# Pre-norm factors moved from the weights to the transposed inputs in a two-layer hybrid decoder kernel, and the high/low weight split made two tiles at a time

## The chip, the core and the metric

The kernel runs on one core of a Trainium2 chip, as one launch. The time is device microseconds (us) of that launch, and the median of several runs is compared. Five engines work beside each other and meet at semaphores: TensorE (PE, matmuls; PEld are its weight loads), VectorE (DVE), ScalarE (ACT), GpSimd (POOL) and SyncE (SP, which here issues the DMAs).

## What is computed

Two layers run one after the other over 256 tokens of 1024 features, all in fp32. A layer has four sub-layers: a SwiGLU FFN, a token mixer (retention heads and gated-linear-attention heads side by side), cross-attention into 256 memory tokens, and a second SwiGLU FFN. Each one is wrapped in two RMSNorms:

```
def rmsnorm(x, g):
    y = x * rsqrt(mean(x * x, axis=-1) + EPS)
    return y * g                          # g: one factor per feature

for l in range(2):
    x = x + 0.5 * rmsnorm(swiglu(rmsnorm(x, ffn1_pre_g[l]), ...), ffn1_post_g[l])
    x = x + rmsnorm(hybrid_mixer(rmsnorm(x, mix_pre_g[l]), ...), mix_post_g[l])
    x = x + rmsnorm(memory_cross_attn(rmsnorm(x, xa_pre_g[l]), rmsnorm(mem, xa_mem_g[l]), ...), xa_post_g[l])
    x = x + 0.5 * rmsnorm(swiglu(rmsnorm(x, ffn2_pre_g[l]), ...), ffn2_post_g[l])
```

The change is about the factors `g` of the norms that stand ahead of a projection: `ffn1_pre_g`, `mix_pre_g`, `xa_pre_g`, `xa_mem_g`, `ffn2_pre_g`, and the per-head norm factors that stand ahead of the mixer's output projection (`G_HEAD`). Since rmsnorm(x, g) @ W is r * (x @ (g * W)) and also r * ((x * g) @ W), with r one number per token, a factor can be multiplied into the rows of W or into the columns of x.

## The kernel before

**Numbers in two parts.** fp32 operands are written as a high part (rounded to the format fp32r) and a low part (the rest), and every product is three matmuls: high x low, low x high and high x high (`three`, L463 to L467). So every weight that streams in is split by two instructions: ACT writes `w_hi` (`split_hi`, L833) and DVE writes `w_lo` = weight minus `w_hi` (`split_lo`, L1153). The same is done to every transposed input: PE transposes 128x128 blocks of x into a PSUM bank `tb` (`transposes`, L516), ACT copies the bank into `xT_hi` (`t_hi`, L864), DVE subtracts and writes `xT_lo` (`t_lo`, L1174).

**Weights.** They come in chunks of 512 output columns by up to 8 blocks of 128 rows, in two halves (h = 0, 1) of 4 blocks (k = 0..3). Four half-sized slots (`raw`, `w_hi`, `w_lo`) are used in turn; SP loads a slot as soon as its split is done. For a chunk behind a norm the factors are in the split: ACT copies each block with a per-partition scale (L858) and DVE multiplies and subtracts in one instruction (L1170), one block of 128x512 at a time, since the factor differs from block to block. For a chunk with no norm ahead of it (FFN down, the attention's output) the split is two blocks at a time, 128x1024 (`pieces`, L852 and L1164). PE waits on `s_lo` for each block, or each pair of blocks.

**Order.** Each engine has one queue written out by hand. PE runs passes: one pass is one chunk by one tile of 128 tokens (t = 0, 1), 24 matmuls of 512 columns. At the seams between sub-layers two chunks are run as a `pair` (L546): first both with t = 0, then both with t = 1, so that tile 0 can start while tile 1 still is being normed. `boundary` (L888 on ACT, L1209 on DVE) is the order there: the square sum of the output (`y_square`), the residual update of tile 0 (`x_update`, L1206), the split of the next chunk's first half, then the copies of the transposed tile 0 (`x_hi`, `x_lo`), then on ACT the square of x (`x_square`, `junk_x` L878) and the second half, then the same for tile 1. POOL does the small per-token arithmetic of the norms in order: `pre` (five to seven operations on 128x1, L1600 to L1607) for the next norm of tile 0, and behind it `post` (L1590 to L1593) for the residual update of tile 1.

**Mixer.** The levels of the gated attention are a chain: POOL forms exponents and decayed keys (L1644, L1645, L1657, L1658), ACT takes the exponential, PE multiplies (`level`, L593), DVE takes the result out (`level_out`). Weight splits stand between them in DVE's queue. For the low-rank gate `w_ga` the factor is multiplied in by an instruction of its own (`w_ga_s`, L1338) ahead of its split.

**Memory.** Behind the mixer's output chunk are the square sum of the memory tokens (L1060), their norm (POOL L1679 and L1680, DVE L1420), and their transposes and copies (`mem_hi`, `mem_lo`).

Of the kernel before, what the change touches and what calls it, by code (L numbers as in the profile page):

```python
# [33 lines left out]
ds = bass.ds  # L34
# [25 lines left out]
def ffn_chunks(f):  # L60
    gain = (G_FFN1, G_FFN2)[f]
    up = [(f"gu{f}", j, 0, 4, gain) for j in range(FU)]
    return up + [(f"down{f}", n, k, nk, None) for n, k, nk in DOWN]
# [4 lines left out]
CHUNKS += [("in", c, 0, 4, G_MIX) for c in range(6)]  # L68
C_OUT = len(CHUNKS)
CHUNKS += [("out", c, 0, 4, G_HEAD) for c in range(2)]  # L70
C_K = len(CHUNKS)
CHUNKS += [("kv", c, 0, 4, G_MEM) for c in range(2)]
C_Q = len(CHUNKS)
CHUNKS += [("q", c, 0, 4, G_XA) for c in range(2)]
C_V = len(CHUNKS)
CHUNKS += [("kv", 2 + c, 0, 4, G_MEM) for c in range(2)]
C_O = len(CHUNKS)
CHUNKS += [("o", c, 0, 4, None) for c in range(2)]
# [44 lines left out]
N_TS = len(SPLIT_USES)  # L123

# [8 lines left out]
def program(nc, a, out):  # L133

    ctx = ExitStack()
    with ctx:
# [29 lines left out]
        w_ga_s = sb("w_ga_s", [P, KD, RANK])  # L166
# [102 lines left out]
        s_tev = sem("transposed_evacuated")  # L269
        s_m = [sem(f"mixer_bank_done{i}") for i in range(2)]  # L270
# [12 lines left out]
        s_gas = sem("w_ga_scaled")  # L283
# [48 lines left out]

        def m_no(l, use):
            return l * N_M + M_USES.index(use) + 1
# [32 lines left out]
        def other(l):  # L367

            return l * -1 + 1

        def weight_src(ci, h, l, j=None):
# [4 lines left out]
            name, col, k0, nk, _ = CHUNKS[ci]  # L376
# [78 lines left out]
        def _(pe):  # L455
# [4 lines left out]
            def wait_split(use, l):  # L460
                pe.wait_ge(s_tev, t_no(l, use) + 1)
# [7 lines left out]
            def token_pass(l, ci, q, t, src_hi, src_lo, k_src=0, first=True, last=True, x_ci=0, x_q=0,  # L469
# [3 lines left out]
                nk, gained = CHUNKS[ci % N_CH][3], CHUNKS[ci % N_CH][4] is not None  # L473
# [3 lines left out]
                for h in range(2):  # L477
# [21 lines left out]
            def column_pass(l, ci, q, t, src_hi, src_lo):  # L499

                wait_acc(l, q, t)
                for mt in range(2):
                    c = (2 * t + mt) * P
                    for h in range(2):
                        slot = (2 * ci + h) % 4
                        for k in range(4):
                            if t == 0 and mt == 0:
                                pe.wait_ge(s_lo, 4 * half_no(l, ci, h) + k + 1)
# [323 lines left out]
        def _(act):  # L832
            def split_hi(l, ci, h, i=None):  # L833

                lay = l
                if ci >= N_CH:
                    lay = other(l)
                _, _, _, nk, gain = CHUNKS[ci % N_CH]
# [25 lines left out]
            def t_hi(l, use, dst, cols=COL, extra=0):  # L864
                act.wait_ge(s_t, t_no(l, use) + 1 + extra)
                act.activation(dst, tb[t_bank(use)][:, 0:cols], ACT.Copy).then_inc(s_thi, 1)

            def x_hi(l, phase, t):
                for g in range(2):
                    t_hi(l, ("x", phase, t, g), xT_hi[:, 4 * g:4 * g + 4, t * P:(t + 1) * P])  # L870
# [102 lines left out]
            def mixer(l):  # L973
# [18 lines left out]
                act.wait_ge(s_gas, l + 1)  # L992
                act.activation(w_ga_hi[:, :, :], w_ga_s[:, :, :], ACT.Copy).then_inc(s_gah, 1)
# [44 lines left out]
                def mix_hi(t):  # L1038
                    for g in range(2):
                        t_hi(l, ("mix", t, g), xT_hi[:, 4 * g:4 * g + 4, t * P:(t + 1) * P])  # L1040
# [7 lines left out]
            def mem_hi(l, t):  # L1048
                for g in range(2):
                    t_hi(l, ("mem", t, g), mT_hi[:, 4 * g:4 * g + 4, t * P:(t + 1) * P])  # L1050
# [84 lines left out]
            for h in range(2):  # L1135
                act.wait_ge(s_raw[h], 16)
                for k in range(4):
                    g = G_FFN1 * KD + 4 * h + k
                    act.activation(w_hi[:, h, k, :], raw[:, h, k, :], ACT.Copy,
                                   scale=gains[:, g:g + 1]).then_inc(s_hi, 1)  # L1140
# [11 lines left out]
        def _(dve):  # L1152
            def split_lo(l, ci, h, i=None):  # L1153

                lay = l
                if ci >= N_CH:
                    lay = other(l)
                _, _, _, nk, gain = CHUNKS[ci % N_CH]
                slot = (2 * ci + h) % 4
                before = 4 * half_no(l, ci, h) + (0 if i is None else i * 16)  # L1160
                if gain is None:
                    for a, b in pieces(nk):
                        dve.wait_ge(s_hi, before + a + 2)
                        dve.tensor_tensor(w_lo[:, slot, a:b, :], raw[:, slot, a:b, :],  # L1164
                                          w_hi[:, slot, a:b, :].bitcast(F32), ALU.subtract).then_inc(s_lo, 2)
                    return
# [639 lines left out]
```

## Time and profile before

| | us |
|---|---|
| three runs | 1245.61, 1245.77, 1248.5 |
| median | 1245.77 |
| the profiled execution: span from the first to the last instruction | 1248.1 |
| its own time (the span and what lies around it) | of the runs only 1248.5 is longer than this span |
| PE busy | 1221.2 (98%) |
| DVE busy | 803.7 (64%) |
| ACT busy | 670.3 (54%) |
| POOL busy | 156.0 (12%) |
| granted TensorE clock, mean | 0.990 |
| chain that ended last | PE 89%, DVE 4%, issue 2%, POOL 2%, ACT 1% |

A matmul's record overlaps the next one's, so "busy" for PE says that its queue had work and not how fast it went; that is read from the distance of the starts. An engine that isn't PE matters only where PE waits for it. The granted clock is at its upper level (1.0, 2.4 GHz) or its lower one (0.50, 1.2 GHz).

### The profile page before, as it was taken

The numbers are of one execution on the slowest core, as the hardware profiler recorded it, in microseconds if no ns is written. First come the engines' busy times: TensorE is split into PE (matmuls) and PEld (weight loads), VectorE is DVE, ScalarE is ACT, GpSimd is POOL, SyncE is SP. The second block draws the span as 40 slices with busy tenths as digits, with TensorE's granted clock in tenths as the row PEclk, the third lists the DMA queues.
The fourth block names the chain that finished last, engine by engine and source line by source line (L and its number), as shares of the span: only waits on it lengthen the run. The fifth ranks groups of instructions, "written<-read, shape, count | busy, mean of one in ns | idle before, by whom it ended". The sixth has DMA issues, their size and how long they took to land.

```text
span 1248.1 us, 19438 instructions
## 1 busy us (share of the span) xinstructions
PE 1221.2 (98%) x6120; PEld 1022.5 (82%) x6120; DVE 803.7 (64%) x1214; ACT 670.3 (54%) x1117; POOL 156.0 (12%) x282
## 2 busy tenths in 40 slices
PE   7999999999999999999999999999999999999997
PEld 5888888787898888888888888877879988888886
DVE  6767546766756576665476665467667556767655
ACT  6555436644655465553465554456457446555444
POOL 1000003642210010000010000037322001000001
PEclk9999999999999999999999999999899999999999
DMA  8556564333553355565465565463345544555563
GB/s 332 202 174 213 193 210 155 135 111 129 184 201 127 123 192 193 177 211 189 157 204 188 182 210 189 157 211 110 102 169 165 167 159 135 203 174 196 181 213 129
DMA packets 32916, 220.06 MB, mean 176 GB/s; under 512 B 4272, under 2 KB 4528, under 8 KB 8768
## 3 DMA queue, kind: packets, MB, share of 16 engines
q1 hardware_dynamic: 32544, 218.98, 51.2%
q8 instruction: 46, 0.75, 0.2%
q14 instruction: 38, 0.31, 0.1%
q10 hardware_dynamic: 288, 0.02, 0.0%
HBM read 217.93 MB, written 1.05 MB: 175 GB/s over the span
## 4 chain that ended last, share of the span: by engine, by line
PE 89%; DVE 4%; issue 2%; POOL 2%; ACT 1%; DMA 0%; DVEq 0%; ACTq 0%; POOLq 0%
PE acc L465 27%; PE acc L467 27%; PE acc L466 26%; PE tb L524 3%; DVE w_lo L1170 2%; PE mb L610 2%; PE acc L762 1%; PE mb L746 1%; PE mb L699 1%; ACT w_hi L858 1%; DVE xT_lo L1176 0%; POOL r_head L1667 0%; DMA inv_f<-in_inv_freq 0%; DVE pg L1304 0%; DVE w_lo L1164 0%
## 5 line engine op out<-in xcount | busy, mean ns | idle before, releaser
L1170 DVE SCALAR_TENSOR_TENSOR w_lo<-raw,gains,w_hi 128x512 fp32r<-128x512 f32 x580 | 418.1, 782 | 47.2 <-ACT w_hi L858 46.1
L465 PE MATMUL acc<-w_hi,xT_hi 128*128 128x512 f32 x1024 | 411.5, 402 | 7.9 <-DVE xT_lo L1176 3.5
L467 PE MATMUL acc<-w_hi,xT_lo 128*128 128x512 f32 x1024 | 402.4, 393 | 0.0
L466 PE MATMUL acc<-w_lo,xT_hi 128*128 128x512 f32 x1024 | 401.6, 392 | 0.0
L858 ACT ACTIVATE w_hi<-raw,gains 128x512 fp32r<-128x512 f32 x580 | 370.0, 714 | 40.7 <-PE acc L467 40.4
L465 PEld LDWEIGHTS acc<-w_hi,xT_hi 128*128 128x128 f32 x1024 | 194.4, 190 | 51.4 <-DVE xT_lo L1176 5.7
L467 PEld LDWEIGHTS acc<-w_hi,xT_lo 128*128 128x128 f32 x1024 | 193.9, 189 | 42.2
L466 PEld LDWEIGHTS acc<-w_lo,xT_hi 128*128 128x128 f32 x1024 | 194.5, 190 | 38.0
L1164 DVE TENSOR_TENSOR w_lo<-raw,w_hi 128x1024 fp32r<-128x1024 f32 x112 | 123.5, 1145 | 72.6 <-ACT w_hi L852 71.9
L923 ACT ACTIVATE th<-acc,r_half 128x256 f32<-128x256 f32 x88 | 41.9, 476 | 197.1 <-PE acc L467 195.3
L852 ACT ACTIVATE w_hi<-raw 128x1024 fp32r<-128x1024 f32 x112 | 105.4, 991 | 77.2 <-PE acc L467 77.2
L465 PE MATMUL acc<-w_hi,hT_hi 128*128 128x512 f32 x352 | 139.3, 396 | 0.0
L467 PE MATMUL acc<-w_hi,hT_lo 128*128 128x512 f32 x352 | 137.9, 392 | 0.0
L466 PE MATMUL acc<-w_lo,hT_hi 128*128 128x512 f32 x352 | 136.8, 389 | 0.0
L1241 DVE SCALAR_TENSOR_TENSOR gt<-th,acc 128x256 f32<-128x256 f32 x88 | 37.0, 421 | 138.8 <-ACT th L923 138.5
L1590 POOL TENSOR_TENSOR v_post<-yss 128x1 f32<-128x1 f32 x16 | 3.1, 194 | 825.5 <-ACT junk_y L885 825.3
L467 PEld LDWEIGHTS acc<-w_hi,hT_lo 128*128 128x128 f32 x352 | 66.1, 188 | 15.4
L466 PEld LDWEIGHTS acc<-w_lo,hT_hi 128*128 128x128 f32 x352 | 66.1, 188 | 14.3
L465 PEld LDWEIGHTS acc<-w_hi,hT_hi 128*128 128x128 f32 x352 | 66.2, 188 | 13.1
L1196 DVE TENSOR_TENSOR yg<-acc,post_gain 128x512 f32<-128x512 f32 x32 | 21.7, 688 | 46.8 <-ACT junk_y L885 46.8
L885 ACT ACTIVATE junk_y<-acc 128x512 bf16<-128x512 f32 x32 | 19.0, 593 | 53.7 <-PE acc L467 53.4
L1244 DVE SCALAR_TENSOR_TENSOR h_tok<-gt,c_half,acc 128x256 f32<-128x256 f32 x88 | 42.3, 481 | 3.1
(175 smaller groups left out, 1264.3 us busy)
## 6 DMA issues: line engine op xcount, KB each, us to landing
raw<-in_gu SPq DMA_DIRECT2D x92, 1024.0 KB, 5.1
raw<-in_down SPq DMA_DIRECT2D x32, 1024.0 KB, 5.0
raw<-in_in SPq DMA_DIRECT2D x24, 1024.0 KB, 5.1
raw<-in_kv SPq DMA_DIRECT2D x16, 1024.0 KB, 5.1
raw<-in_down SPq DMA_DIRECT2D x16, 768.0 KB, 4.2
raw<-in_out SPq DMA_DIRECT2D x8, 1024.0 KB, 5.2
raw<-in_q SPq DMA_DIRECT2D x8, 1024.0 KB, 5.1
raw<-in_o SPq DMA_DIRECT2D x8, 1024.0 KB, 5.1
```

The lines of the kernel that those rows point to most:

```text
L465: pe.matmul(o, st_hi, mv_hi, start=first, stop=False)
L466: pe.matmul(o, st_hi, mv_lo, start=False, stop=False)
L467: return pe.matmul(o, st_lo, mv_hi, start=False, stop=last)
L524: mm = pe.transpose(tb[t_bank(use)][0:rows, lo:lo + w], src, ident[:, :])
L610: mm = pe.matmul(mb[e][:, c:c + 64], tile, later, start=True, stop=True)
L852: act.activation(w_hi[:, slot, a:b, :], raw[:, slot, a:b, :], ACT.Copy).then_inc(s_hi, 2)
L858: act.activation(w_hi[:, slot, k, :], raw[:, slot, k, :], ACT.Copy, scale=gains[:, ds(g, 1)]).then_inc(s_hi, 1)
L923: act.activation(th[:, t, :], acc[(q0 + j) % 2][t][:, 0:256], ACT.Tanh, scale=r_half[:, t:t + 1]).then_inc(s_tanh, 1)
L1164: dve.tensor_tensor(w_lo[:, slot, a:b, :], raw[:, slot, a:b, :], w_hi[:, slot, a:b, :].bitcast(F32), ALU.subtract).then_inc(s_lo, 2)
L1170: dve.scalar_tensor_tensor(w_lo[:, slot, k, :], raw[:, slot, k, :], gains[:, ds(g, 1)], w_hi[:, slot, k, :].bitcast(F32), ALU.mult, ALU.su ...
L1241: dve.scalar_tensor_tensor(gt[:, t, :], th[:, t, :], 1.0, b[:, 0:256], ALU.add, ALU.mult).then_inc(s_gated, 1)
L1244: dve.scalar_tensor_tensor(h_tok[:, j % 2, t, :], gt[:, t, :], c_half[:, t:t + 1], b[:, 256:512], ALU.mult, ALU.mult).then_inc(s_accf[bank ...
```

## The change

The factors leave the weights. A transposed input now goes through three instructions where there were two: DVE multiplies the PSUM bank by the factors into a part of the buffer `yg` (`gained`), ACT copies that into the high part (`gained_hi`), DVE subtracts (`gained_lo`). DVE does both banks of a tile first and both subtractions after (`gained_pair`). ACT's copy waits for DVE's multiplication and not for PE any more. All weight splits are now without factors and two blocks at a time. PE waits for inputs on a new semaphore (`s_split`), and for the weights in pairs of blocks. `w_ga_s` is gone. The second layer's factors of the first FFN are chosen by `x_gain`.

```diff
@@ tensor @@
-                pe.wait_ge(s_tev, t_no(l, use) + 1)
+                if use in GAIN_USES or use[:3] == ("x", 0, 0):
+                    pe.wait_ge(s_split, tg_no(l, use) + 1)
+                else:
+                    pe.wait_ge(s_tev, t_no(l, use) + 1)
...
-                        if t == 0 and (gained or k in (0, 2)):
-
-                            step = k + 1 if gained else k + 2
-                            pe.wait_ge(s_lo, 4 * half_no(l, ci, h) + 4 * x_ci + step)
+                        if t == 0 and k in (0, 2):
+
+                            pe.wait_ge(s_lo, 4 * half_no(l, ci, h) + 4 * x_ci + k + 2)
@@ scalar @@
-                if gain is None:
-                    for a, b in pieces(nk):
-                        act.activation(w_hi[:, slot, a:b, :], raw[:, slot, a:b, :], ACT.Copy).then_inc(s_hi, 2)
-                    return
-
-                act.nop(nofuse=True)
-                for k in range(nk):
-                    g = lay * (N_GAINS * KD) + gain * KD + h * nk + k
-                    act.activation(w_hi[:, slot, k, :], raw[:, slot, k, :], ACT.Copy,
-                                   scale=gains[:, ds(g, 1)]).then_inc(s_hi, 1)
+                for a, b in pieces(nk):
+                    act.activation(w_hi[:, slot, a:b, :], raw[:, slot, a:b, :], ACT.Copy).then_inc(s_hi, 2)
...
+            def gained_hi(l, use, dst):
+
+                act.wait_ge(s_tev, t_no(l, use) + 1)
+                act.activation(dst, xg(use), ACT.Copy).then_inc(s_thi, 1)
@@ vector @@
-                for k in range(nk):
-                    dve.wait_ge(s_hi, before + k + 1)
-                    g = lay * (N_GAINS * KD) + gain * KD + h * nk + k
-                    dve.scalar_tensor_tensor(w_lo[:, slot, k, :], raw[:, slot, k, :], gains[:, ds(g, 1)],
-                                             w_hi[:, slot, k, :].bitcast(F32), ALU.mult,
-                                             ALU.subtract).then_inc(s_lo, 1)
+                for a, b in pieces(nk):
...
+            def gained(l, use, kind):
...
+                dve.wait_ge(s_t, t_no(l, use) + 1)
+                dve.tensor_tensor(xg(use), tb[t_bank(use)][:, :].rearrange("p (k n) -> p k n", k=4),
+                                  gains[:, col].unsqueeze(2).to_broadcast([P, 4, P]), ALU.mult).then_inc(s_tev, 1)
+
+            def gained_lo(l, use, dst, hi):
+
+                dve.wait_ge(s_thi, ts_no(l, use) + 1)
+                dve.tensor_tensor(dst, xg(use), hi.bitcast(F32), ALU.subtract).then_inc(s_split, 1)
+
+            def gained_pair(l, uses, kind, dst, hi, t):
+                for use in uses:
+                    gained(l, use, kind)
+                for use in uses:
+                    g = use[-1]
+                    s = (slice(None), slice(4 * g, 4 * g + 4), slice(t * P, (t + 1) * P))
+                    gained_lo(l, use, dst[s], hi[s])
...
             def x_lo(l, phase, t):
-                for g in range(2):
-                    s = (slice(None), slice(4 * g, 4 * g + 4), slice(t * P, (t + 1) * P))
-                    t_lo(l, ("x", phase, t, g), xT_lo[s], xT_hi[s])
+                gained_pair(l, [("x", phase, t, g) for g in range(2)], x_gain(l, phase), xT_lo, xT_hi, t)
...
-                g_mix = gains[:, ds(l * (N_GAINS * KD) + G_MIX * KD, KD)].unsqueeze(2).to_broadcast([P, KD, RANK])
-                dve.tensor_tensor(w_ga_s[:, :, :], w_ga[:, ds(l, 1), :, :].rearrange("p o k n -> p (o k) n"), g_mix,
-                                  ALU.mult).then_inc(s_gas, 1)
...
             def mix_out(l):
...
                 mem_lo(l, 1)
+
+                dve.wait_ge(s_split, tg_no(l, ("mem", 1, 1)) + 1)
                 y_gain(l, 1, Q_OUT, 0, 1)
```

At the seam from the first FFN to the mixer, ACT's queue before has this behind the first half of the next chunk (`tb` is the PSUM bank, `junk_x` the square of x that POOL's `pre` waits for):

```order
L866 ACTIVATE xT_hi<-tb 128x4x128 [waits transposed]
...
L878 ACTIVATE junk_x,xss<-x 128x1024 [waits x_squared,x_ready]
L849 REGISTER_ALU [waits raw_loaded3]
L858 ISA [waits pass_done]
L858 ACTIVATE w_hi<-raw,gains 128x512
...
L885 ACTIVATE junk_y,yss<-acc 128x512 [waits y_squared,pass_done]
```

and after the change:

```order
L876 ACTIVATE xT_hi<-yg 128x4x128 [waits transposed_evacuated]
...
L888 ACTIVATE junk_x,xss<-x 128x1024 [waits x_squared,x_ready]
L862 REGISTER_ALU [waits raw_loaded3]
L864 ACTIVATE w_hi<-raw 128x1024 [waits pass_done]
L864 ACTIVATE w_hi<-raw 128x1024
L867 REGISTER_ALU
L895 ACTIVATE junk_y,yss<-acc 128x512 [waits y_squared,pass_done]
```

The copy of the transposed tile (left out: the second one of the same form) keeps its place and now waits for DVE's `transposed_evacuated`; the square of x stays behind it. DVE's queue at the same seam before, from the copies of tile 0 to the residual update of tile 1:

```order
L1176 TENSOR_TENSOR xT_lo<-tb,xT_hi 128x4x128 [waits transposed_hi_copied]
...
L1170 ISA [waits w_hi_ready]
L1170 SCALAR_TENSOR_TENSOR w_lo<-raw,gains,w_hi 128x512
...
L1196 TENSOR_TENSOR yg<-acc,post_gain 128x512 [waits y_squared]
L1201 REGISTER_ALU
L1206 SCALAR_TENSOR_TENSOR x<-yg,r_post,x 128x512 [waits acc_free1,r_post_ready]
```

and after the change:

```order
L1182 TENSOR_TENSOR yg<-tb,gains 128x512
...
L1188 TENSOR_TENSOR xT_lo<-yg,xT_hi 128x4x128 [waits transposed_hi_copied]
...
L1168 TENSOR_TENSOR w_lo<-raw,w_hi 128x1024 [waits w_hi_ready]
...
L1213 TENSOR_TENSOR yg<-acc,post_gain 128x512 [waits y_squared]
...
L1223 SCALAR_TENSOR_TENSOR x<-yg,r_post,x 128x512 [waits acc_free1,r_post_ready]
```

Two instructions (one for each bank) now stand ahead of the two subtractions, and four weight instructions became two. Between the mixer and its output projection DVE's queue after the change reads as follows; before, the `yg<-tb,gains` rows weren't there and each `w_lo` row stood for half as many blocks:

```order
L1352 TENSOR_TENSOR o_sb<-o_sb,gate 128x512 [waits heads_normed,acc_free1]
...
L1168 TENSOR_TENSOR w_lo<-raw,w_hi 128x1024 [waits w_hi_ready]
...
L1182 TENSOR_TENSOR yg<-tb,gains 128x512 [waits transposed]
...
L1188 TENSOR_TENSOR xT_lo<-yg,xT_hi 128x4x128 [waits transposed_hi_copied]
...
L1430 TENSOR_SCALAR mem_t<-mem_t,r_mem 128x1024 [waits r_mem_ready]
```

## Rows read from the trace of the kernel before

**Rows 1.** The page's first part: busy time, share of the span and instructions.
```profile
PE 1221.2 (98%) x6120; PEld 1022.5 (82%) x6120; DVE 803.7 (64%) x1214; ACT 670.3 (54%) x1117; POOL 156.0 (12%) x282
```

**Rows 2.** PE's waits: waited for; us in total, times, longest (one of eight).
```profile
PE acc L465 <- DVE xT_lo L1176: 3.5, 2, 1.8
```

**Rows 3.** Timeline, FFN up: start, us, engine line op out<-in, count.
```profile
60.24 0.39 PE L467 MATMUL acc<-w_hi,xT_lo 128*128 128x512 f32 x1
60.47 0.39 PE L465 MATMUL acc<-w_hi,xT_hi 128*128 128x512 f32 x1
```

**Rows 4.** Timeline, split without factors, 128x1024, on DVE and on ACT.
```profile
128.44 2.36 DVE L1164 TENSOR_TENSOR w_lo<-raw,w_hi 128x1024 fp32r<-128x1024 f32 x2
...
127.28 2.00 ACT L852 ACTIVATE w_hi<-raw 128x1024 fp32r<-128x1024 f32 x2
```

**Rows 5.** Timeline, the start; in brackets the idle time and its releaser.
```profile
8.48 1.29 DVE L1176 TENSOR_TENSOR xT_lo<-tb,xT_hi 128x512 fp32r<-128x512 f32 x2
...
10.48 0.79 PE L465 MATMUL acc<-w_hi,xT_hi 128*128 128x512 f32 x1 [3.48 <-DVE w_lo L1551]
```

**Rows 6.** Timeline, seam from the first FFN to the mixer.
```profile
196.38 1.06 ACT L878 ACTIVATE junk_x<-x 128x1024 bf16<-128x1024 f32 x1
...
198.28 2.74 DVE L1170 SCALAR_TENSOR_TENSOR w_lo<-raw,gains,w_hi 128x512 fp32r<-128x512 f32 x4 [0.96 <-ACT w_hi L858]
...
199.15 0.60 POOL L1604 TENSOR_SCALAR r<-r_pre 128x1 f32<-128x1 f32 x1
...
202.79 1.41 DVE L1206 SCALAR_TENSOR_TENSOR x<-yg,r_post,x 128x512 f32<-128x512 f32 x2 [1.17 <-POOL r_post L1593]
204.12 2.73 DVE L1170 SCALAR_TENSOR_TENSOR w_lo<-raw,gains,w_hi 128x512 fp32r<-128x512 f32 x4
...
205.22 0.39 PE L465 MATMUL acc<-w_hi,xT_hi 128*128 128x512 f32 x1
```

**Rows 7.** Timeline, inside the mixer.
```profile
235.18 8.80 DVE L1170 SCALAR_TENSOR_TENSOR w_lo<-raw,gains,w_hi 128x512 fp32r<-128x512 f32 x8
...
239.15 0.72 PE L602 MATMUL mb<-gqk 64*128 64x128 f32 x8 [0.22 <-POOL gqk L1658]
...
244.46 1.57 PE L610 MATMUL mb<-gqk 64*128 64x64 f32 x16 [1.62 <-DVE pgx L1293]
```

**Rows 8.** Timeline, from the mixer to the output projection and the memory tokens.
```profile
302.63 2.72 DVE L1170 SCALAR_TENSOR_TENSOR w_lo<-raw,gains,w_hi 128x512 fp32r<-128x512 f32 x4
...
306.01 0.50 PE L465 MATMUL acc<-w_hi,xT_hi 128*128 128x512 f32 x1 [1.77 <-DVE xT_lo L1176]
...
310.48 2.56 ACT L858 ACTIVATE w_hi<-raw,gains 128x512 fp32r<-128x512 f32 x4
...
315.98 1.09 PE L524 MATMUL tb<-ident,mem_t 128*128 128x128 f32 x8 [0.61 <-DVE mem_t L1420]
```

**Rows 9.** Timeline: attention to second FFN, then from layer 0 to layer 1.
```profile
442.86 3.40 DVE L1170 SCALAR_TENSOR_TENSOR w_lo<-raw,gains,w_hi 128x512 fp32r<-128x512 f32 x5
...
444.80 0.39 PE L465 MATMUL acc<-w_hi,xT_hi 128*128 128x512 f32 x1
...
630.65 2.73 DVE L1170 SCALAR_TENSOR_TENSOR w_lo<-raw,gains,w_hi 128x512 fp32r<-128x512 f32 x4
...
632.03 0.39 PE L465 MATMUL acc<-w_hi,xT_hi 128*128 128x512 f32 x1
...
634.53 2.74 DVE L1170 SCALAR_TENSOR_TENSOR w_lo<-raw,gains,w_hi 128x512 fp32r<-128x512 f32 x4 [1.15 <-ACT w_hi L858]
```

**Rows 10.** Timeline of DVE at the end of the program.
```profile
1243.57 1.42 DVE L1206 SCALAR_TENSOR_TENSOR x<-yg,r_post,x 128x512 f32<-128x512 f32 x2 [0.88 <-POOL r_post L1593]
```

**Rows 11.** Stretches: PE, PEld, DVE, ACT, POOL busy (instructions), granted clock, DMA share, GB/s.
```profile
243.10:246.50 3.40, 2.04 (x21) 2.00 (x22) 2.33 (x5) 1.42 (x3) 3.25 (x5) 1.00 0.60 186
246.50:249.90 3.40, 3.40 (x13) 2.81 (x11) 3.24 (x5) 2.76 (x5) 3.32 (x5) 0.50 0.50 212
304.60:308.00 3.40, 1.99 (x9) 1.64 (x10) 3.37 (x7) 3.29 (x6) 0.00 (x0) 1.00 1.03 429
```

More of the change, by code:

```diff
@@ L60, in ffn_chunks @@
 def ffn_chunks(f):
-    gain = (G_FFN1, G_FFN2)[f]
-    up = [(f"gu{f}", j, 0, 4, gain) for j in range(FU)]
-    return up + [(f"down{f}", n, k, nk, None) for n, k, nk in DOWN]
+    up = [(f"gu{f}", j, 0, 4) for j in range(FU)]
+    return up + [(f"down{f}", n, k, nk) for n, k, nk in DOWN]
 CHUNKS = ffn_chunks(0)
 C_IN = len(CHUNKS)
-CHUNKS += [("in", c, 0, 4, G_MIX) for c in range(6)]
+CHUNKS += [("in", c, 0, 4) for c in range(6)]
 C_OUT = len(CHUNKS)
-CHUNKS += [("out", c, 0, 4, G_HEAD) for c in range(2)]
+CHUNKS += [("out", c, 0, 4) for c in range(2)]
 C_K = len(CHUNKS)
-CHUNKS += [("kv", c, 0, 4, G_MEM) for c in range(2)]
+CHUNKS += [("kv", c, 0, 4) for c in range(2)]
 C_Q = len(CHUNKS)
-CHUNKS += [("q", c, 0, 4, G_XA) for c in range(2)]
+CHUNKS += [("q", c, 0, 4) for c in range(2)]
 C_V = len(CHUNKS)
-CHUNKS += [("kv", 2 + c, 0, 4, G_MEM) for c in range(2)]
+CHUNKS += [("kv", 2 + c, 0, 4) for c in range(2)]
 C_O = len(CHUNKS)
-CHUNKS += [("o", c, 0, 4, None) for c in range(2)]
+CHUNKS += [("o", c, 0, 4) for c in range(2)]
 C_FFN2 = len(CHUNKS)
@@ L123 @@
 N_TS = len(SPLIT_USES)
+GAIN_USES = [u for u in SPLIT_USES if u[0] != "h"]
+N_TG = len(GAIN_USES)
 LEVELS = [128, 64, 32, 16, 8, 4, 2, 1]
@@ L282, in program @@
         s_rope_t = sem("rope_table_ready")
-        s_gas = sem("w_ga_scaled")
         s_gah = sem("w_ga_hi_ready")
@@ L329, in ts_no, with x_gain, xg, tg_no @@
             return l * N_TS + SPLIT_USES.index(use) + 2
+        def x_gain(l, phase):
+            return (l, (G_FFN1, G_MIX, G_XA, G_FFN2)[phase]) if phase < 4 else (other(l), G_FFN1)
+        def xg(use):
+            t = 1 if use[0] == "mem" else use[-2]
+            return yg[:, t, use[-1] * COL:(use[-1] + 1) * COL].rearrange("p (k n) -> p k n", k=4)
+        def tg_no(l, use):
+            if use[0] == "x" and use[1:3] == (0, 0):
+                return l * N_TG + use[3]
+            return l * N_TG + GAIN_USES.index(use) + 2
         def m_no(l, use):
@@ L833, in split_hi @@
             def split_hi(l, ci, h, i=None):
[L835 to L838, printed above, removed]
+                nk = CHUNKS[ci % N_CH][3]
                 slot = (2 * ci + h) % 4
@@ L991, in split_after @@
                         split_hi(l, ci + 2, 0)
-                act.wait_ge(s_gas, l + 1)
-                act.activation(w_ga_hi[:, :, :], w_ga_s[:, :, :], ACT.Copy).then_inc(s_gah, 1)
+                act.activation(w_ga_hi[:, :, :], w_ga[:, ds(l, 1), :, :].rearrange("p o k n -> p (o k) n"),
+                               ACT.Copy).then_inc(s_gah, 1)
                 split_hi(l, C_IN + 1, 1)
@@ L1136, in _ @@
                 act.wait_ge(s_raw[h], 16)
[L1137 to L1140, printed above, removed]
+                for k0, k1 in pieces(4):
+                    act.activation(w_hi[:, h, k0:k1, :], raw[:, h, k0:k1, :], ACT.Copy).then_inc(s_hi, 2)
             x_square(0, 0, 0)
@@ L1153, in split_lo @@
             def split_lo(l, ci, h, i=None):
[L1155 to L1158, printed above, removed]
+                nk = CHUNKS[ci % N_CH][3]
                 slot = (2 * ci + h) % 4
                 before = 4 * half_no(l, ci, h) + (0 if i is None else i * 16)
[L1161 to L1166, printed above, removed]
-                for k in range(nk):
-                    dve.wait_ge(s_hi, before + k + 1)
-                    g = lay * (N_GAINS * KD) + gain * KD + h * nk + k
-                    dve.scalar_tensor_tensor(w_lo[:, slot, k, :], raw[:, slot, k, :], gains[:, ds(g, 1)],
-                                             w_hi[:, slot, k, :].bitcast(F32), ALU.mult,
-                                             ALU.subtract).then_inc(s_lo, 1)
+                for a, b in pieces(nk):
+                    dve.wait_ge(s_hi, before + a + 2)
+                    dve.tensor_tensor(w_lo[:, slot, a:b, :], raw[:, slot, a:b, :],
+                                      w_hi[:, slot, a:b, :].bitcast(F32), ALU.subtract).then_inc(s_lo, 2)
             def t_lo(l, use, dst, hi, extra_t=0, extra_s=0):
@@ L1412, in mem_lo @@
             def mem_lo(l, t):
-                for g in range(2):
-                    s = (slice(None), slice(4 * g, 4 * g + 4), slice(t * P, (t + 1) * P))
-                    t_lo(l, ("mem", t, g), mT_lo[s], mT_hi[s])
+                gained_pair(l, [("mem", t, g) for g in range(2)], (l, G_MEM), mT_lo, mT_hi, t)
             def mix_out(l):
@@ L1546, in _ @@
             x_lo(0, 0, 0)
-            for h in range(2):
-                for k in range(4):
-                    dve.wait_ge(s_hi, 4 * h + k + 1)
-                    g = G_FFN1 * KD + 4 * h + k
-                    dve.scalar_tensor_tensor(w_lo[:, h, k, :], raw[:, h, k, :], gains[:, g:g + 1],
-                                             w_hi[:, h, k, :].bitcast(F32), ALU.mult, ALU.subtract).then_inc(s_lo, 1)
+            split_lo(0, 0, 0)
+            split_lo(0, 0, 1)
             split_lo(0, 1, 0)
```

31 lines of the change are left out of this document (16 added, 15 removed).

## The prediction

> **What bounds the kernel now.** Read the page's first part first: PE is busy for 98% of the span, DVE for 64%, ACT for 54% [rows 1]. Then see whether PE really runs: in an FFN's up stage its matmuls start 0.23 us apart [rows 3], and that distance holds through all FFN passes; no wait of PE falls in them. So the weight splits there, most of DVE's and ACT's work, lie beside PE and are worth nothing. What is left is PE's idle time, 27 us of 1248, and it has places: the start, where 3.48 us end with the first split [rows 5], the inside of the mixer [rows 7], and the way from the mixer to the memory tokens [rows 8]; PE's list of waits says the same, with 1.8 us twice for a transposed tile [rows 2]. The third thing to read is how near the other seams are to a wait. At the seam from the first FFN to the mixer the first block of the pass that starts at 205.22 is split by about 204.9 [rows 6]: 0.35 us of cover. At the layer's end it is 631.4 against 632.03, and ahead of the second FFN 443.6 against 444.80 [rows 9].
>
> **The change, part by part.** The steady state first. Four blocks of a half chunk take DVE 2.73 us now [rows 6] and 2.36 in two pieces [rows 4]; ACT 2.56 [rows 8] and 2.00 [rows 4]. Over the 588 factored blocks that is about 54 us of DVE and 80 us of ACT less, all under PE's passes: 0 us. What remains is the added step of each transposed tile, and the first piece, which is ready 1.22 us after its start instead of 0.75 (a two-piece row's 2.36 less a pitch of 1.14). The added multiplication is priced by the subtraction it resembles, two in 1.29 us [rows 5], 0.64 each.
>
> What a tile's path does now: ACT and DVE overlap on two banks. After: both multiplications on DVE, then ACT's copies, then both subtractions. More important, ACT's copies now stand behind whatever DVE has queued, and everything behind them on ACT waits too. For each place I lay the queues out again with these durations.
>
> *Start.* DVE is free at 8.4. Two multiplications end at 9.7, ACT's second copy (0.6) at 10.4, ACT's first weight piece (1.05) at 11.3, DVE's first piece 1.22 later at 12.6. PE begins at 12.7 instead of 10.48 [rows 5]: **+2.2**. Nothing behind it catches up, since PE is the bound.
>
> *Seam to the mixer, once a layer.* Tile 0 itself is early enough. But ACT's square of x, at 196.38 [rows 6], can start only behind the copies: DVE ends the first half's split at 196.0, multiplies until 197.3, ACT copies until 197.8, so +1.4. POOL's chain for the next norm hangs on that square, and POOL's chain for the residual update of tile 1 stands behind it. While DVE splits, POOL's operations on 128x1 take 0.60 each [rows 6] where undisturbed ones take 0.19; with two pieces of 1.14 fewer of them are caught, but each for longer, and the last runs later: another +0.3. So the update moves from 202.79 to about 204.5, the split behind it from 204.12 to 205.83, and its first piece is ready at 207.05 where PE wants it at 205.22: 1.83 of wait. Tile 1's copies, for which PE now loses 0.3 at 212, then come in time, since the next half chunk is split earlier (ACT no longer waits for `w_ga_s`). Net 1.55, twice: **+3.1**.
>
> *Mixer.* Eight factored blocks take DVE 8.80 us there, 1.1 each instead of 0.68, because POOL works on its exponents at the same time [rows 7]. The Trainium skill, page "SBUF — State Buffer", section "SBUF: two separate sides", says that VectorE with two SBUF inputs and GpSimd take a shared port pair in turn, each for a whole instruction. The trace agrees as far as the 1.1 goes. If instead both were merely slowed in proportion, the shorter splits would release the later PE wait some 0.8 us sooner, and the whole sum would be 1.6 lower.
>
> By taking turns, counted in the mixer's queues: POOL's first decayed keys come 0.6 later (PE waits for them at 239.15), the splits end 0.9 sooner, and PE's wait at 244.46 then ends on POOL at about 244.3. Net -0.15, twice: **-0.3**.
>
> *Mixer to memory tokens, once a layer.* DVE splits from 302.63. In two pieces that ends at 304.9; multiplications until 306.2; ACT's first copy in between until 306.25; the subtraction until 307.0. PE starts at 307.05 instead of 306.01 [rows 8]: +1.04. Then gate, product, split and tile 1: DVE's multiplications end at 312.5, ACT's copies at 313.1, so ACT's next split starts there and not at 310.48, and is 0.56 shorter. The memory's square sum, norm and transposes follow it: PE transposes at 318.05 instead of 315.98. Together +2.05 a layer, twice: **+4.1**. Behind it the queues run 1 us late, but the column passes cover that.
>
> *Attention to the second FFN.* The square of x is 1.3 later, but POOL was free for 0.3 of it: the update is 1.0 later, the first piece ready at 445.1 against 444.80: +0.35, twice: **+0.7** (bounds 0 and 0.9).
>
> *Layer 0 to layer 1, once.* As in the seam to the mixer: first piece at 630.65 + 1.7 + 1.22 = 633.6 against 632.03 [rows 9]: 1.6. The next split waits 1.15 us in the loop's return, now at 634.53 and then at 636.2, which moves as the branch does; it covers itself but for 0.2. Tile 1's multiplications come behind it, and its last subtraction ends 1.0 after PE wants it (0.16 now). **+2.7**.
>
> *End.* The last residual update is at 1243.57 [rows 10], behind the same ACT and POOL chain: **+1.75**. The output's DMA and the last splits follow.
>
> Sum: 2.2 + 3.1 - 0.3 + 4.1 + 0.7 + 2.7 + 1.75 = 14.25 us.
>
> **The clock.** In the stretch from 243.1 to 246.5 PE is busy for 2.04 us of 3.40, mostly with 64-column matmuls, and in the next one the granted clock is 0.50: 13 matmuls in 3.4 us. In 304.6 to 308.0 it is busy for 1.99 us and the clock stays at 1.0 [rows 11]. Such half-speed stretches (1.2 GHz) stand at the same three places of both layers and cost about 1.5 us each. The change lengthens the idle at 304 to 307 from 1.8 to 2.8 us, makes new waits of 1.6 to 1.9, and delays the first matmuls at the start, where PE also runs at half clock until 14.4. Bounds for the net: three fewer (-4.5) and five more (+7.5). I take one more, +1.5, since PE's idle grows and nowhere shrinks by much, and rows 11 show that 1.4 us of idle alone was not enough. The sum becomes 15.75.
>
> The page "TensorE: Matmul & The Clock Gate" of the Trainium skill, section "Part 1: The HAM clock gate", says the activity monitor runs free of the program's start. By that rule the same idle time costs in one run and not in another. No row here shows it, and one trace cannot.
>
> The sum stands against the profiled execution (span 1248.1, near the run of 1248.5). The median of the runs is 2.3 below that span; the added waits don't depend on which of them is meant, so I add them to the median: 1245.8 + 15.75 = 1261.5, said as **1262**.
>
> **The rivals.**
> - *The clock follows every longer wait.* Five more half-speed stretches instead of one: 14.25 + 7.5, 1267.5. For it: the idle of 2.8 us at 304, and four new waits of 1.6 and more. Against it: at 304 to 307 PE is caught up later by the memory's wait anyway. Chance 0.15.
> - *Only the two multiplications count.* If POOL and ACT do not carry the delay on to tile 1, each of eight seams and ends costs the 1.3 us added on DVE less the 0.4 to 0.5 saved in the split: about 7, so 1253. For it: cover of 0.35 to 1.2 at three of four kinds of seam. Against it: the order above puts the square of x behind the copies. Chance 0.13.
> - *Nothing moves.* Each added step lies in slack I did not see: within 3.7 us of 1245.8. It is also where a change that moved no wait would land. Against it: the start alone costs 2.2, with nothing ahead of PE. Chance 0.06.
> - *Faster: the mixer decides.* There a wait of 1.62 us, 0.22 ahead of it, and a half-speed stretch of 1.5 hang on DVE's and POOL's turns. If shorter splits freed both, 3.3 us a layer come back, 6.6 in all: 1239 if the seams cost nothing. It decides only when the seams cost under 6.6 together, against the 14.5 above. Chance 0.04.
> - The forecast, 1257 to 1266: 0.62.
>
> **The range.** 1252 to 1270 takes in the rival of the multiplications, the bounds of the small terms, and most of the clock's. What a measurement of this kernel can tell from no change is about 0.3%, 3.7 us. Faster than that 0.04, within it 0.07, slower 0.89.
>
> **What would show it.** Right: PE's first matmul of the first pass near 12.7; a PE wait of 1.8 for `w_lo` in the second pass behind each first FFN; the wait for the transposed tile at the output projection grown from 1.77 to 2.8 and the one for `mem_t` from 0.6 to near 1.9; FFN passes still at 0.23 us a matmul; the last residual update 1.7 later behind PE's last matmul. Wrong: if the seam's wait is absent, POOL's chain did not carry the delay; if the excess is in stretches with a granted clock of 0.50, the clock is the cause and not the queues; if the FFN passes are slower than 0.23, the longer instructions take something from PE that no row shows.

## The result

The changed kernel takes 1261.38 us (median of 4 runs, 1259.46 to 1261.93), the kernel before 1247.13 beside it (1245.61 to 1251.11): ratio 1.0102, interval 1.0074 to 1.0129. It is slower by 14.25 us. The forecast was 1262, range 1252 to 1270.

The page of the changed kernel gives, as [rows 1] for before:

```profile
PE 1219.0 (97%) x6120; PEld 1018.7 (81%) x6120; DVE 776.8 (62%) x968; ACT 592.1 (47%) x823; POOL 168.4 (13%) x282
```

ACT is busy 78 us less and DVE 27 us less, and the kernel is slower: neither was the bound. What counts is PE's list of waits (engine, line, waited for: us in total, times, longest), to be laid beside [rows 2]:

```profile
PE acc L482 <- DVE w_lo L1168: 10.6, 6, 5.7
PE acc L482 <- DVE xT_lo L1188: 5.8, 3, 2.8
PE tb L540 <- DMA gains<-in_gains: 5.2, 1, 5.2
PE tb L540 <- DVE mem_t L1430: 2.2, 2, 1.1
PE mb L626 <- POOL gqk L1666: 1.9, 2, 1.0
PE mb L618 <- POOL gqk L1666: 1.8, 2, 0.9
```

Before, waits for `w_lo` were 3.5 us at the start and 0.7 in two other places; now they are 10.6, in six places (5.7 of it at the start). Waits for a transposed tile grew from 3.5 to 5.8.

The new seam from the first FFN to the mixer, in the timelines of ACT, POOL, DVE and PE (start, us, engine line op, count, idle time before and its releaser; before: [rows 6]). PE stands 2.6 us later than in the kernel before by then, so 2.6 is to be taken off each start:

```profile
200.18 1.04 ACT L888 ACTIVATE junk_x<-x 128x1024 bf16<-128x1024 f32 x1
...
202.37 2.36 DVE L1168 TENSOR_TENSOR w_lo<-raw,w_hi 128x1024 fp32r<-128x1024 f32 x2 [1.37 <-ACT w_hi L864]
...
202.45 1.20 POOL L1611 TENSOR_SCALAR r<-r_pre 128x1 f32<-128x1 f32 x1 [0.16 <-POOL r_pre L1609]
203.70 1.07 POOL L1612 TENSOR_SCALAR r<-r_pre 128x1 f32<-128x1 f32 x1
204.84 0.19 POOL L1613 TENSOR_SCALAR n<-r_pre 128x1 f32<-128x1 f32 x1
...
207.00 1.42 DVE L1223 SCALAR_TENSOR_TENSOR x<-yg,r_post,x 128x512 f32<-128x512 f32 x2 [1.67 <-POOL r_post L1601]
...
209.60 0.50 PE L482 MATMUL acc<-w_hi,xT_hi 128*128 128x512 f32 x1 [1.62 <-DVE w_lo L1168]
```

Read it from the top: the square of x is 1.2 later, two of POOL's scalings are held for 1.20 and 1.07 us behind DVE's 128x1024 subtractions, the residual update is 1.6 later, and PE waits 1.62 for the first piece. The forecast had 1.4 for the square, 1.7 for the update and 1.8 for the wait.

**Where the 14 us are.** The traces of before and after differ by 9.6 us of span only, not 14.25. Every run lists its span and its mean granted clock, and over the more than 150 runs of this study the span of any one kernel rises by 1.06 us for each 0.001 of clock that is missing, with a scatter of 0.6. So each kernel has a span extrapolated to full clock (what its queues cost) and a part that the clock adds:

```
kernel (runs)          median   span at full clock   added by the clock (mean)
before (64)            1247.6        1238.2                8.0
changed kernel (10)    1261.9        1250.2               10.4
```

The queues cost 12.0 us, the clock 2.4, give or take 0.7 by the scatter of the runs. "At full clock" means these spans in what follows; with four to six runs they are good to some 0.3 to 0.5. The first of the two columns is some 2 us too low and the second too high by as much: the clock's record is at its lower level also behind PE's last matmul (4.9 and 4.7 us in the two traces of before, 6.2 and 4.2 in those of the changed kernel), where it costs nothing. In a difference between two kernels most of this drops out.

### The profile page after: what moved, and what is told of

Read it like the earlier page. It is cut to its first block, busy times and chain, and to the rows that moved or that the text cites. A ratio compares the mean times of both kernels' runs of the same rounds, so it can differ in the third digit from the quotient of the medians.

```text
span 1257.7 us, 18476 instructions
## 1 busy us (share of the span) xinstructions
PE 1219.0 (97%) x6120; PEld 1018.7 (81%) x6120; DVE 776.8 (62%) x968; ACT 592.1 (47%) x823; POOL 168.4 (13%) x282
## 4 chain that ended last, share of the span: by engine, by line
PE 86%; DVE 4%; POOL 3%; ACT 3%; issue 3%; DMA 0%; DVEq 0%; ACTq 0%; POOLq 0%
PE acc L482 26%; PE acc L484 26%; PE acc L483 26%; PE tb L540 3%; ACT w_hi L864 2%; PE mb L626 2%; DVE w_lo L1168 2%; PE acc L778 1%; PE mb L762 1%; DVE yg L1182 1%; POOL gqk L1665 0%; POOL gqk L1666 0%; ACT junk_x L888 0%; POOL o_sb L1652 0%; POOL o_sb L1653 0%
## 5 line engine op out<-in xcount | busy, mean ns | idle before, releaser
L1168 DVE TENSOR_TENSOR w_lo<-raw,w_hi 128x1024 fp32r<-128x1024 f32 (+1 forms) x406 | 483.5, 1233 | 134.0 <-ACT w_hi L864 128.6
L864 ACT ACTIVATE w_hi<-raw 128x1024 fp32r<-128x1024 f32 (+1 forms) x402 | 394.9, 1034 | 116.8 <-PE acc L484 116.1
L482 PE MATMUL acc<-w_hi,xT_hi 128*128 128x512 f32 x1024 | 411.6, 402 | 16.7 <-DVE w_lo L1168 10.6
L876 ACT ACTIVATE xT_hi<-yg 128x512 fp32r<-128x512 f32 x42 | 25.8, 632 | 75.3 <-DVE yg L1182 75.3
L482 PE MATMUL acc<-xT_hi,w_hi 128*128 128x256 f32 x128 | 36.6, 286 | 0.0
```

The costliest lines, as they stand in the source:

```text
L482: pe.matmul(o, st_hi, mv_hi, start=first, stop=False)
L876: act.activation(dst, xg(use), ACT.Copy).then_inc(s_thi, 1)
```

## Experiments

**The clock and the start: both kernels once more.** No edit; first the kernel before.

> The kernel before, unchanged, for a second trace beside these. If the half-speed stretches follow from the kernel's own idle time, they stand at the same places (246.5, 273.8, 287.5 and the same in layer 1) and the span is within 0.5 of 1248.1. If they depend on something outside the program, their places or number differ and the span moves by about 1.4 us for each one more or fewer.

Measured: 1247.04, span of the trace 1243.4 against 1248.1. There are two half-speed stretches ahead of the end instead of six. These two (286.4 and 897.4) stand beside the same matmuls as two of the six; the other four are absent. Stretches of this second trace (us; PE, PEld, DVE, ACT, POOL busy and instructions; granted clock, DMA share, GB/s), to lay beside [rows 11]:

```profile
243.10:246.50 3.40, 1.77 (x11) 1.20 (x9) 3.21 (x5) 0.39 (x1) 3.32 (x4) 1.00 0.70 267
246.50:249.90 3.40, 3.40 (x29) 3.12 (x29) 2.48 (x5) 3.15 (x6) 3.32 (x6) 1.00 0.87 296
...
286.42:289.83 3.41, 3.41 (x10) 2.62 (x10) 3.41 (x6) 0.00 (x0) 0.00 (x0) 0.50 0.02 5
```

PE idles in the first stretch as it did in [rows 11], but nothing behind it runs at half speed. By 254 PE has gained 1.6 on the first trace. The same queue pattern is paid for in one run and not in another. This agrees with what the Trainium skill says, page "TensorE: Matmul & The Clock Gate", section "Part 1: The HAM clock gate": the activity monitor runs free of the program's start.

The start differs too:

```profile
10.12 3.22 ACT L1139 ACTIVATE w_hi<-raw,gains 128x512 fp32r<-128x512 f32 x5 [1.02 <-DMA raw<-in_gu]
...
11.68 0.79 PE L465 MATMUL acc<-w_hi,xT_hi 128*128 128x512 f32 x1 [4.40 <-DVE w_lo L1551]
```

In this run the first weights landed at 10.1 and PE began at 11.68, not at 10.48 as in [rows 5].

The changed kernel once more, also without an edit:

> The changed kernel, unchanged, for a second trace and more runs of it. If the half-speed stretches of the clock hang on something outside the program, they stand at other places than 288.9, 309.4, 906.7 and 927.2, and their number moves by one or more; PE's waits are the same to 0.1 us but for the start, where the landing of the first weights moves by about 1 us. If they hang on the kernel alone, places and span (1257.7) repeat.

Measured: 1263.15 (6 runs), span of the trace 1262.5 against 1257.7. The seams' waits for weights repeat (the list gives 10.6 in six places again), the slow stretches do not (7 now where the first trace has 4). Two waits moved by more than the 0.1 expected, both beside a stretch that moved: those for transposed tiles, 6.3 for 5.8, and those for `mem_t`, 2.8 for 2.2. In all twelve traces of this study every slow stretch ahead of the end lies in the mixer or on the way from it to the memory tokens (246 to 313 us in layer 0, 855 to 933 in layer 1), none in an FFN; which of these places are hit differs from run to run. So the clock's part can only be given as a mean, and what is left when it is taken out is a property of the kernel.

**Each half of the change alone.**

The weights one block at a time again, the factors on the inputs (the code in this section is abridged):

```
-  for a, b in pieces(nk):                       # pairs, 128x1024
+  for a, b in (blocks_of(nk) if single(ci) else pieces(nk)):   # 128x512 in the factored chunks
```

> The changed kernel with its factors on the transposed input, but the weights of the factored chunks split one 128x512 block at a time again (the down and `o` chunks stay in pairs, as in the kernel before). It does the input half of the change alone. If the added step on the transposed tiles carries the cost (queues): the first block is ready 0.75 after its start and not 1.22, but a half chunk takes DVE 0.37 longer, so each of the eight places gets back 0.1 to 0.4 us; the time is 1258 to 1261, 11 to 14 above the kernel before. If the late first piece of the pairs is the cause: most of it comes back and the time is 1247 to 1252.

The weights in pairs without the multiplications. This kernel leaves the factors out altogether, so it computes something else; its time stands for the weight half:

```
-  gained(l, use, kind) ... gained_lo(l, use, dst[s], hi[s])
+  t_lo(l, use, dst[s], hi[s])                   # no multiplication; ACT copies from the bank
```

> The changed kernel without its multiplications: the transposed tiles are copied and subtracted straight from their banks as in the kernel before, weights in pairs. The factors of the four input norms and of the head and memory norms are left out altogether, so this is the weight half of the change alone. Queues: the start +0.5, the seams within 0.3 of before, the mixer 0.5 a layer shorter (DVE and ACT free sooner); the time is within 2 us of the kernel before. If the pairs are the cause: 5 us or more above the kernel before.

Measured: input half alone 1258.57, at full clock 1246.1, 7.9 above before. Weight half alone 1247.07, at full clock 1238.9, 0.7 above before: ratio 0.9996, 0.9982 to 1.0010. "The pairs are the cause" falls. But the halves add up to 8.6 and the change costs 12.0: 3.4 us come only from both together. Offsets of PE's matmuls against the first trace of before show where (us lost in that place, minus for gained; half-speed stretches left out, so the output projection and memory can be given only for a trace and layer without one there, for the changed kernel its second trace):

```
place                        forecast  changed   input alone   weights alone
seam to the mixer, layer 0     1.55      1.32        0.18           0.12
seam to the mixer, layer 1     1.55      1.29        0.21           0.11
output proj. and memory        2.05      2.04        2.35          -0.75
attention to second FFN        0.35      0.39        0.0            0.0
layer 0 to layer 1             2.7     1.7, 2.5      2.3            0.1
end                            1.75      1.61        0.58           0.42
```

At the seams to the mixer, behind the attention and at the end the halves sum to 0.3, 0.3, 0 and 1.0, and the change costs 1.3, 1.3, 0.4 and 1.6. There is a cover (time by which a piece is ready before PE wants it) of 0.35 [rows 6] that each half alone can use, and something more. The single blocks show part of it:

```profile
202.47 0.52 POOL L1620 TENSOR_SCALAR r<-r_pre 128x1 f32<-128x1 f32 x1
...
205.91 1.41 DVE L1231 SCALAR_TENSOR_TENSOR x<-yg,r_post,x 128x512 f32<-128x512 f32 x2 [1.16 <-POOL r_post L1609]
```

POOL's scaling waits 0.52 here behind a 128x512 subtraction and 1.20 in the changed kernel behind a 128x1024 one, while undisturbed ones take 0.19; its five scalings take 2.3 us here and 3.1 there, and the update comes 1.1 earlier. Before they took 2.7, with the weight half alone 3.1. So each half alone moves the update by little (0.5 and 0.4 later), and both together by 1.6: by these rows, of the 1.0 that this seam costs beyond the two halves, 0.35 is the cover and some 0.6 this chain, 0.4 of it in the scalings. In eight traces looked through, every such operation of POOL that was held ended within 0.1 us of the end of the DVE instruction it met, as it would if the two took turns for whole instructions: the Trainium skill, page "SBUF — State Buffer", section "SBUF: two separate sides", says so, and the traces agree at both lengths.

There is a second finding in the groups by form (line, op, count | busy, mean ns of one). Single blocks without a factor are not as slow as those of before with one:

```profile
L1176 DVE TENSOR_TENSOR w_lo<-raw,w_hi 128x512 fp32r<-128x512 f32 x604 | 400.7, 724 | 36.0 <-ACT w_hi L871 32.5 <-issue 1.9 <-DMA w_ga<-in_w_ga 1.2
L871 ACT ACTIVATE w_hi<-raw 128x512 fp32r<-128x512 f32 x596 | 326.2, 620 | 36.5 <-PE acc L491 36.3
```

In queue they follow each other at 0.60 on DVE and 0.52 on ACT, where [rows 6] gave 0.66 on DVE (2.74 for four) and the factored copies of before 0.61 on ACT. Four blocks take DVE 2.49 us so, against 2.74 with the factor and 2.36 in two pieces. Two thirds of what the change saves on DVE in a half chunk come from the factor that is gone, one third from the pairing, which makes the first piece 0.54 later.

**The chain through POOL.** First the square ahead of the copies, then POOL's own order.

```
-  x_hi(l, phase + 1, 0)
   x_square(l, phase + 1, 0)
+  x_hi(l, phase + 1, 0)
```

> The changed kernel with one order changed: at a seam ACT takes the square sum of the new x ahead of the two copies of the transposed tile, in the gap in which it waits for DVE's multiplications. Queues: POOL's chain starts 1.4 earlier, so PE's waits for the first piece in the second pass behind the first FFN (1.8) and at the start of layer 1 (1.5) fall to under 0.5, attention to second FFN to 0, and the last residual update comes 1.4 earlier: together 5 to 7 us, 1254 to 1256. If POOL's chain does not carry the delay (only DVE's two multiplications count): under 1 us, 1260 to 1262.

Measured: 1255.68, at full clock 1243.4, 6.8 below the changed kernel. POOL's scalings now run ahead of the splits, and the update waits for little:

```profile
196.34 1.04 ACT L888 ACTIVATE junk_x<-x 128x1024 bf16<-128x1024 f32 x1
...
198.78 0.19 POOL L1611 TENSOR_SCALAR r<-r_pre 128x1 f32<-128x1 f32 x1 [0.16 <-POOL r_pre L1609]
...
204.30 1.42 DVE L1223 SCALAR_TENSOR_TENSOR x<-yg,r_post,x 128x512 f32<-128x512 f32 x2 [0.47 <-POOL r_post L1601]
```

PE has no wait left in this seam; in layer 0 it even gains 0.6 there on the kernel before (0.4 in layer 1), since the tile copies come in time as well. The medians show the gain (6.2 us); the spans of single traces don't (1256.2 with 8 slow stretches, against 1257.7 with 4).

```
   then(r_pre = v_pre ** -0.5)            # shortened
+  post(l, *between)          # residual factor of tile 1, ahead of r_8, r_16, n_16, r_half, c_half
```

> The changed kernel with one order changed on POOL: at the seams from FFN to mixer, from attention to the second FFN, from layer to layer and at the end, the three short operations of the residual's norm factor for tile 1 go ahead of the five scalings of the next norm's factor. If the long splits of DVE that hold these scalings up (1.2 and 1.1 us for operations that take 0.2 undisturbed) are what makes both halves of the change together dearer than their sum (11.9 us against 7.9 and 0.6), the residual update comes 1.5 earlier and the waits behind it go at all five places: 5 to 7 us below the changed kernel, 1256 to 1258. If the cost lies in DVE's own queue (multiplications and a late first piece), under 2 us: 1260 and more.

Measured: 1258.23, at full clock 1246.0, 4.2 below the changed kernel: under the 5 to 7 expected, well over the 2 of the rival.

```profile
204.22 0.92 POOL L1598 TENSOR_TENSOR v_post<-yss 128x1 f32<-128x1 f32 x1 [1.57 <-ACT junk_y L895]
...
208.76 0.50 PE L482 MATMUL acc<-w_hi,xT_hi 128*128 128x512 f32 x1 [0.41 <-DVE w_lo L1168]
```

The wait for the first piece falls from 1.62 to 0.41. The rest is that the first of the three operations now waits for ACT's square sum of the output (1.57 idle) and is then itself caught behind a long subtraction (0.92 instead of 0.19). So POOL's five scalings ahead of the update are on the path that PE waits for. How much of the 4.2 is their longer holding and how much is the plain order (they take time undisturbed, too) isn't shown: no run has this order with single blocks or in the kernel before.

**The memory's norm.** Square sums ahead of `mix_hi(1)` on ACT, scaling ahead of `split_lo(l, C_OUT + 1, 1)` on DVE.

> The changed kernel with the memory's square sums taken on ACT ahead of the copies of the head outputs' second tile (ACT is idle there from 310.3 to 313.8) and its scaling on DVE ahead of the last split of the `out` weights. Queues: the transposes of the memory follow PE's matmuls without a wait (1.5 us a layer between the last matmul and them now), and the split behind has 1.4 of cover: 2 to 3 us below the changed kernel. If the scaling only pushes the split behind it onto PE: within 1 us of the changed kernel.

Measured: 1260.74 (median; mean 1260.0), at full clock 1248.5, 1.7 below the changed kernel. The transposes stand without a wait:

```profile
319.72 1.04 PE L540 MATMUL tb<-ident,mem_t 128*128 128x128 f32 x8
```

That place gains 1.3 in layer 0, but 0.4 of it is given back inside the attention, between 345 and 358; the seam to the second FFN costs its 0.39 as without the edit. A little under what was expected.

**All orders together, on both kernels.** Four orders are changed: the square of x ahead of the copies, the memory's norm early (the edits of the two experiments above), the rope tables' copies behind the first splits at the start, and one of the two pieces of the `out` chunk's second half ahead of the last gate product. The last two:

```
   split_lo(0, 0, 1)
+  rope_c, rope_s copies                 # were ahead of x_lo(0, 0, 0)
+  split_lo(l, C_OUT, 1, part=0)
   mixed(5, 0)
-  split_after(10)
+  split_lo(l, C_OUT, 1, part=1)
```

> The changed kernel with four orders changed, no operation added: the squares of x ahead of the copies (as in e3), the memory's norm early (as in e6), the rope tables' copies behind the first splits at the start, and on DVE one of the two pieces of the second half of the first `out` chunk ahead of the last gate product. Queues: 7 + 2.5 + 1 (start, now bound by the landing of the weights) + 0.8 (output projection) = 11 us below the changed kernel, 1249 to 1252. If the waits only move on to the next late step: 1254 and more.

> The kernel before with the same four orders as in e7. Queues: the seams get back the 0.3 of the tile copies, the memory 0.6 to 1 a layer, the output projection 0.4 a layer, the start at most 0.4: 2 to 4 us below the kernel before, 1243 to 1246, and below e7 by 4 us and more, since the added multiplications remain there. If the multiplications were the only thing wrong with the change and the reorder hides them, e7 comes to within 1 us of this one or below it.

Measured: changed kernel reordered 1250.31, at full clock 1240.0; kernel before reordered 1245.93, at full clock 1234.7 (ratio to before 0.9983, 0.9963 to 1.0004: the times alone don't tell it from before, the 3.5 us show at full clock). The reorder takes 10.2 us off the changed kernel, and between the two reordered kernels 5.3 us are left: 1.1 to 1.7 at the start, 1.5 a layer at the output projection, 1.0 between the layers. At the projection the tile's path has no cover, since its input is the last thing to be ready:

```profile
306.93 0.50 PE L482 MATMUL acc<-w_hi,xT_hi 128*128 128x512 f32 x1 [2.47 <-DVE xT_lo L1188]
```

**A version better than both.** In [rows 7] PE waits for `pgx`, the first level's products, whose copy on DVE stands behind eight splits. In e8's kernel it goes ahead of the last four:

```
+  level_out(0)
   split_after(4)
-  level_out(0)
```

> The kernel of e8 (before, reordered) with one more order changed on DVE: inside the mixer the two copies of the first level's products (0.4 us each) go ahead of the four splits of the fourth projection's second half instead of behind them. Queues: PE's second level no longer waits for DVE (1.6 us a layer) but for POOL's decayed keys, which end 0.5 us ahead of the copies now: 1 us a layer, 2 us below e8, so 1243 to 1245 and clearly below the kernel before. If POOL's operations come later because DVE's order moves under them, nothing is gained against e8.

Measured: 1240.02 (10 runs), before 1249.26 beside it: ratio 0.9928, 0.9902 to 0.9954. At full clock 1232.2, 6.0 below before and 2.5 below the reordered kernel (2 expected). That the time fell under the 1243 expected, and 9 below the runs beside it, is in part the clock: its part is 6.0 here, 8.6 in the reordered kernel and 8.9 in the runs of before beside it.

```profile
240.50 0.75 DVE L1293 COPY pgx<-mb 128x256 f32<-128x256 f32 x2 [0.25 <-PE mb L602]
...
243.71 1.60 PE L610 MATMUL mb<-gqk 64*128 64x64 f32 x16 [0.29 <-POOL gqk L1659]
```

The wait of 1.6 is 0.3, and it now ends on POOL. This better version owes nothing to the change: its factors are in the weights.

## Why the prediction was right

**FFN passes: right.** No wait of PE falls in them, and 27 and 78 us less of DVE and ACT bring nothing.

**Start: mechanism right, term too large.** PE starts at 12.85 (12.7 forecast):

```profile
8.58 1.28 DVE L1182 TENSOR_TENSOR yg<-tb,gains 128x512 f32<-128x512 f32 x2
...
12.85 0.79 PE L482 MATMUL acc<-w_hi,xT_hi 128*128 128x512 f32 x1 [5.66 <-DVE w_lo L1168]
```

But +2.2 was taken from a run of before in which the weights landed at 8.8. In the other trace they landed at 10.1 and before started 1.2 later, while the changed kernel's splits start at 10.4 and do not care. Over two traces of each, at the matmuls of 35 us, the change costs 1.3. Not foreseen was a loss of 0.45 at 26.65 in the first trace, where tile 1's copies come late.

**Seam to the mixer: right** (1.32 and 1.29 for 1.55), by the chain forecast. The 0.3 for POOL "caught" behind longer pieces was the right mechanism and slightly too small: the five scalings took 3.1 us against 2.7. The square of x came 1.2 later for the 1.4 forecast.

**Mixer: right.** PE meets the keys 0.7 later and gains 0.7 at the next wait: 0 for -0.15, and the wait ends on POOL as said:

```profile
243.78 0.72 PE L618 MATMUL mb<-gqk 64*128 64x128 f32 x8 [0.92 <-POOL gqk L1666]
...
248.40 1.60 PE L626 MATMUL mb<-gqk 64*128 64x64 f32 x16 [0.95 <-POOL gqk L1666]
```

The weight half alone shows the same 0.7 and -0.7, so this is the pairs' doing.

**Mixer to memory tokens: right.** The first wait grew from 1.77 to 2.75 (forecast 2.8), the place costs 2.04 where no slow stretch disturbs it (2.05). The memory's wait was 1.1 and not 1.9 in the first trace; a slow stretch stood just ahead of it in both layers (309.3 and 927.2) and gave the queues time. In the second trace it was 1.7 in the layer without one:

```profile
308.00 0.50 PE L482 MATMUL acc<-w_hi,xT_hi 128*128 128x512 f32 x1 [2.75 <-DVE xT_lo L1188]
...
320.07 1.09 PE L540 MATMUL tb<-ident,mem_t 128*128 128x128 f32 x8 [1.10 <-DVE mem_t L1430]
```

**Attention to the second FFN: right** (0.39 for 0.35).

**Layer 0 to layer 1: too large.** Forecast 2.7, measured 1.7 and 2.5 in the two traces. The first piece costs what was said; here PE in the first trace, then DVE's next split in the first and the second:

```profile
638.01 0.50 PE L482 MATMUL acc<-w_hi,xT_hi 128*128 128x512 f32 x1 [1.33 <-DVE w_lo L1168]
...
639.70 2.36 DVE L1168 TENSOR_TENSOR w_lo<-raw,w_hi 128x1024 fp32r<-128x1024 f32 x2 [0.60 <-issue]
```
```profile
641.02 2.36 DVE L1168 TENSOR_TENSOR w_lo<-raw,w_hi 128x1024 fp32r<-128x1024 f32 x2 [1.34 <-issue]
```

The term that was mis-sized is "+1.0 for tile 1's last subtraction": 0.1 and 0.7. It hangs on DVE's idle time between its last split of layer 0 and its first of layer 1, read as the return in the loop, which I took as the 1.15 us of one trace [rows 9] (0.99 in the second of before); it took 0.60 and 1.34. The row names ACT for the 1.15, but ACT had that block ready 2.4 us earlier, so the reading as DVE's own time stands.

**End: right** (1.61 for 1.75). In the trace of after:

```profile
1253.13 1.42 DVE L1223 SCALAR_TENSOR_TENSOR x<-yg,r_post,x 128x512 f32<-128x512 f32 x2 [1.38 <-POOL r_post L1601]
```

**Clock: right in sign, a little small.** +2.4 (give or take 0.7) in the mean against +1.5 for one stretch more; the runs' clocks stand for about 1.6 more. Why the changed kernel has more of them no run shows. The queues' sum was 14.25 and is 12.0 (the places above add up to 12.5): 0.9 of that is the start, 0.6 the way between the layers, 0.5 the two seams to the mixer, the rest small. Queues 2.2 too dear and clock 0.9 too cheap stand against each other, so the total of 15.75 came nearer to the 14.25 measured than its parts did.

**The base.** The trace of before (1248.1) had six slow stretches where the mean run has about four (by its clock, the end left out); a run's time is 2.0 above its span, so it was a run of 1250, not one near 1248.5. Adding the sum to the median and not to the trace was sound. But the median of those three runs was 1.8 below that of all 64, while the sum was 1.5 too large. That the forecast of 1262 met the 1261.4 so closely is luck in part.

## What to carry to other kernels

When PE is the bound, an operation added to the path of a tile is paid at every seam that has too little cover for it, and work saved on the helper engines is worth nothing where PE doesn't wait for it; find the few places with no cover and put the new step's followers (here a square sum that needs only x) ahead of it. Longer instructions on DVE held up POOL's tiny ones until they ended (0.5 to 0.6 us beside 128x512, 1.1 to 1.2 beside 128x1024): count a scalar chain on POOL by the length of what DVE runs beside it. Two steps that lean on the same cover don't both fit into it (0.7 and 7.9 us alone, 12.0 as one), so lay out the queues for the whole change.

## What the runs showed of the hardware

The same program had two half-speed stretches ahead of its end in one trace and six in another, each worth 1.4 to 1.6 us by the offsets of PE's matmuls, always in the mixer or on the way to the memory tokens, but not always in the same of these places. The one at 246.5 came although PE's longest wait ahead of it was 1.6 us. The median of a few runs can be 2 us off from this (1245.8 for three, 1247.6 for all), and one trace 5. Differences of 1 us between kernels came out only from spans compared at equal clock. The landing of the first megabyte of weights varied from 7.8 to 10.1 us over the traces (8.8 and 10.1 in the two of before), which decides what a change at the start costs. And leaving the per-partition factor out of a 128x512 subtraction saves 0.06 us of 0.66 on DVE, out of the copy on ACT 0.09 of 0.61.
